# Reordering the borders of block two: squares, sums and sigmoids ahead of splits, another free bank, low parts by halves of features

## The reference

```python
for i in range(2):
    g = norm_gains[i]
    f = swiglu(rmsnorm(h, g[0]), ffn_gate[i,0], ffn_up[i,0], ffn_down[i,0])   # 1024 -> 2816 -> 1024
    h = h + 0.5 * rmsnorm(f, g[1])
    mix = hybrid_mixer(rmsnorm(h, g[2]), ...)      # latent attention (8 heads) and dilated attention (8 heads), w_in, w_out
    h = h + rmsnorm(mix, g[3])
    f = swiglu(rmsnorm(h, g[4]), ffn_gate[i,1], ffn_up[i,1], ffn_down[i,1])
    h = h + 0.5 * rmsnorm(f, g[5])
    gate = sigmoid(rmsnorm(h, g[6]) @ w_ple_gate[i])
    h = h + rmsnorm((p[i] @ w_ple[i]) * gate, g[7])
```

## Time and profile before

| | us |
|---|---|
| median of 3 runs | 2384.09 (2383.19 to 2384.39) |
| the profiled execution's own time | 2383.87 |
| its span, first to last instruction | 2382.6 |
| TensorE busy | 2034.6 (85%) |
| VectorE busy | 959.8 (40%) |
| ScalarE busy | 649.8 (27%) |
| POOL busy | 63.6 (3%) |
| DMA, mean over the span | 272 GB/s |

### The profile page before, as it was taken

One profiled execution on the slowest core, in us unless ns is written; L12 is line 12 of the kernel. 1 busy time (PEld: TensorE's weight loads), 2 busy tenths in 40 slices (PEclk: granted clock), 3 DMA queues, 4 the chain that ended last, 5 costly groups with the idle time before them and its releaser, 6 DMA issues.

```text
span 2382.6 us, 29091 instructions
## 1 busy us (share of the span) xinstructions
PE 2034.6 (85%) x12318; PEld 1354.3 (57%) x12318; DVE 959.8 (40%) x1181; ACT 649.8 (27%) x779; POOL 63.6 (3%) x144
## 2 busy tenths in 40 slices
PE   7999999676666666766688999989999999999998
PEld 4767862111111111111147998769998999778997
DVE  3735431000000000000005656865657666865656
ACT  3423210000000000000004444444444444454434
POOL 0000000000000000000001001000001000000000
PEclk8999999777777777677799999999999999999999
DMA  7345789999999999999995564235554555315552
GB/s 297 119 183 206 280 362 421 420 421 420 420 421 420 420 421 420 421 420 420 421 420 227 191 213 139 107 117 178 200 177 153 192 189 185 128 63 177 201 182 95
DMA packets 91361, 647.46 MB, mean 272 GB/s; under 512 B 10144, under 2 KB 10656, under 8 KB 14304
## 3 DMA queue, kind: packets, MB, share of 16 engines
q1 hardware_dynamic: 91232, 645.61, 69.3%
HBM read 644.52 MB, written 1.05 MB: 271 GB/s over the span
## 4 chain that ended last, share of the span: by engine, by line
PE 53%; DMA 34%; DVE 8%; SPq 2%; ACT 2%; issue 1%; POOL 1%; DVEq 0%; ACTq 0%; POOLq 0%
PE PS L429 13%; PE PS L431 13%; PE PS L430 13%; DMA ring<-in_md 6%; DMA ring<-in_mu 6%; SPq L2704 2%; DMA XT<-in_mu 2%; DMA ahead<-in_mu 2%; PE PS L913 2%; DVE low L1790 2%; PE PS L818 1%; PE PS L784 1%; DMA HRI<-in_md 1%; DMA QT<-in_md 1%; DMA mix<-in_md 1%; DMA XT<-in_md 1%
## 5 line engine op out<-in xcount | busy, mean ns | idle before, releaser
L1790 DVE TENSOR_TENSOR low<-ring,WH 128x2048 fp32r<-128x2048 f32 (+1 forms) x164 | 374.3, 2283 | 189.2 <-ACT WH L2142 186.2
L429 PE MATMUL PS<-XH,WH 128*128 128x256 f32 x1408 | 398.8, 283 | 6.2 <-DVE XL L1808 6.0
L430 PE MATMUL PS<-XL,WH 128*128 128x256 f32 x1408 | 396.9, 282 | 0.0
L431 PE MATMUL PS<-XH,low 128*128 128x256 f32 x1408 | 394.9, 280 | 0.0
L2142 ACT ACTIVATE WH<-ring 128x2048 fp32r<-128x2048 f32 (+1 forms) x164 | 313.1, 1909 | 24.8 <-DMA ring<-in_fg 19.6
L429 PEld LDWEIGHTS PS<-XH,WH 128*128 128x128 f32 x1408 | 266.6, 189 | 10.3 <-issue 8.5
L431 PEld LDWEIGHTS PS<-XH,low 128*128 128x128 f32 x1408 | 269.3, 191 | 0.0
L430 PEld LDWEIGHTS PS<-XL,WH 128*128 128x128 f32 x1408 | 266.5, 189 | 1.4
L1772 DVE TENSOR_TENSOR T1S<-T1S,PS 128x512 f32<-128x512 f32 x16 | 11.0, 688 | 535.9 <-PE PS L878 535.9
L2392 ACT ACTIVATE T1S<-PS 128x512 f32<-128x512 f32 x16 | 9.6, 598 | 546.7 <-PE PS L878 546.6
L878 PE MATMUL PS<-ring,big 128*32 128x512 f32 x616 | 99.7, 748 | 47.1 <-DMA ring<-in_mu 26.9
(11 more groups left out here) (434 smaller groups left out, 3019.9 us busy)
## 6 DMA issues: line engine op xcount, KB each, us to landing
ring<-in_fg SPq DMA_DIRECT2D x44, 1024.0 KB, 4.9
ring<-in_fu SPq DMA_DIRECT2D x44, 1024.0 KB, 4.9
ring<-in_fd SPq DMA_DIRECT2D x44, 1024.0 KB, 4.8
ring<-in_md SPq DMA_DIRECT2D x43, 1024.0 KB, 27.1
ring<-in_mu SPq DMA_DIRECT2D x39, 1024.0 KB, 27.1
ring<-in_mg SPq DMA_DIRECT2D x38, 1024.0 KB, 27.5
ring<-in_wmod SPq DMA_DIRECT2D x24, 1024.0 KB, 6.2
ahead<-in_mg SPq DMA_DIRECT2D x14, 1024.0 KB, 27.4
```

Source lines behind the costliest of these rows:

```text
L429: t.matmul(o, l[0], r[0], start=start, stop=False, skip_group_check=True)
L430: t.matmul(o, l[0], r[1], start=False, stop=False, skip_group_check=True)
L431: return t.matmul(o, l[1], r[0], start=False, stop=stop, skip_group_check=True)
L1790: own(v.tensor_tensor(low[:, w.slot.index, 0:size], w.flat, WH[:, w.slot.index, 0:size].bitcast(f32), ALU.subtract).then_inc(*c.wl.up()), ...
```

## The change

Nothing is computed otherwise; instructions change places in the lists of four engines, with the counts that they wait for.

- Entry, first ffn: ScalarE splits the third tile between its pairs of squares, VectorE right after the products with ROW, the fourth after the factors. TensorE does the product with DG after the second fg tile (first ffn only). The normalised residual is written in step 2 of the ffn. The split of the first fd tile by VectorE goes behind the hidden tile's low part.
- Ffn to mixer: the residual's add comes before the next split and this before the rows on VectorE; ScalarE squares acc(1) before the second split and XR after it. The first dilated product uses bank 0 in place of 6, dilated keys bank 6 in place of 0, kv_up banks 0 and 1 in place of 6 and 7. VectorE does latent(1) before the first rope and the eviction for KT before the second.
- Mixer to ffn: ScalarE squares XR and acc(1) before the second split, the EM copies are spread between, the last behind the high rows; VectorE makes the add of m = 1 before the factor of m = 0 and the second split.
- Gate to the third ffn (l = 0): gains, high rows and sigmoids alternate, the low rows are taken in the order (m, half) (0,0), (1,0), (0,1), (1,1), the first of them between the product and the Newton step of the add; both factors come last; 6 fillings in place of 8.

The diff, cut to its core:

```diff
@@ tensor_program, ffn
-                        if n == 0:
-                            b = (2 * (1 + p) + 1) % 4
+                            if (n, j) == ((0, 1) if f else (1, 0)):
+                                b = (2 * (1 + p) + 1) % 4
...
@@ mixer
-                    x = part(6, 512, 0, j, "wid", 6 * l + j)
+                    x = part(0, 512, 0, j, "wid", 6 * l + j)
...
-                held[6], held[7] = [(c.ds, 4 * l + 1)], [(c.ds, 4 * l + 2)]
+                held[0], held[7] = [(c.ds, 4 * l + 1)], [(c.ds, 4 * l + 2)]
...
-                dilated(1, 0, 0)
+                dilated(1, 0, 6)
+                held[6] = [(c.ds, 4 * l + 3)]
...
-                kv_up(0, 6)
+                kv_up(0, 0)
...
@@ gate
-                    turn_over(4, 8)
+
+                    turned[0, 1], turned[1, 0] = turned[1, 0], turned[0, 1]
+                    held[1], held[2] = held[2], held[1]
+                    turn_over(4, 6)
@@ vector_program: newton, low_rows and factor take ahead=1 for nth(count, ahead); add also meanwhile
-                newton(m)
+                if meanwhile is not None:
+                    meanwhile()
+                newton(m, ahead=ahead)
...
-            for m in range(2):
-                V.wait_ge(c.rw, 2 * m + 2)
...
+            split_to(4)
+
+            def normed_residual():
...
@@ ffn
-                        split_to(tile("fu", 11 * f + n) + 4)
+                        if f or n:
+                            split_to(tile("fu", 11 * f + n) + 4)
...
+                        split_to(tile("fu", 11 * f + n) + 4)
+                        if f == 0 and n == 2:
+                            normed_residual()
@@ mixer
                 add(0, acc(0), 0.5, 4 * l + 1, 22 * l + 9)
+                split_to(tile("wid", 6 * l) + 1)
                 rows(0, 0, gT[:, g0 + 8:g0 + 16])
+                add(1, acc(1), 0.5, 4 * l + 1, 22 * l + 10)
+                split_to(tile("wid", 6 * l) + 2)
                 rows_factor(0)
-                split_to(tile("wid", 6 * l) + 1)
-                add(1, acc(1), 0.5, 4 * l + 1, 22 * l + 11)
-                split_to(tile("wid", 6 * l) + 2)
                 rows(1, 2, gT[:, g0 + 8:g0 + 16])
...
                 rows_factor(1)
-                dilated(0, 0, 6)
                 split_to(tile("wid", 6 * l) + 3)
                 latent(1)
+                dilated(0, 0, 0)
                 split_to(tile("wid", 6 * l) + 4)
-                dilated(0, 1, 7)
...
-                dilated(1, 0, 0)
+                dilated(0, 1, 7)
+                dilated(1, 0, 6)
@@ mixer to ffn
-                for m in range(2):
-                    add(m, acc(m), 1.0, 4 * l + 2, 22 * l + 19 + 2 * m)
-                    if m == 0:
-                        split_to(tile("fg", 22 * l + 11) + 1)
-                    rows(m, 0, gT[:, g0 + 16:g0 + 24])
-                    w, s = factor(2 + m)
-                    spread(m, w, s)
-                    split_to(tile("fg", 22 * l + 11) + 2 + m)
+                add(0, acc(0), 1.0, 4 * l + 2, 22 * l + 19)
+                split_to(tile("fg", 22 * l + 11) + 1)
+                rows(0, 0, gT[:, g0 + 16:g0 + 24])
+                add(1, acc(1), 1.0, 4 * l + 2, 22 * l + 21, 2)
+                w, s = factor(2, 0)
+                spread(0, w, s)
+                rows(1, 0, gT[:, g0 + 16:g0 + 24])
+                split_to(tile("fg", 22 * l + 11) + 2)
+                w, s = factor(3)
+                spread(1, w, s)
+                split_to(tile("fg", 22 * l + 11) + 3)
@@ gate
+                    for j in range(2):
+                        gains(0, j, j, gT[:, 40:48])
+                gated(1, 1)
                 if l == 0:
-                    rows(0, 0, gT[:, 40:48])
-                    w, s = factor(2)
-                    spread(0, w, s)
-                gated(1, 1)
-                add(1, XN[:, 1, :], 1.0, 4 * l + 4)
-                if l == 0:
-                    rows(1, 2, gT[:, 40:48])
-                    w, s = factor(3)
-                    spread(1, w, s)
+                    add(1, XN[:, 1, :], 1.0, 4 * l + 4, meanwhile=lambda: low_rows(0, 0, 0))
+                    for j in range(2):
+                        gains(1, j, 2 + j, gT[:, 40:48])
+                    low_rows(1, 0, 2, 2)
+                    low_rows(0, 1, 1, 0)
+                    low_rows(1, 1, 3)
+                    for m in range(2):
+                        w, s = factor(2 + m)
+                        spread(m, w, s)
+                else:
+                    add(1, XN[:, 1, :], 1.0, 4 * l + 4)
@@ scalar_program: entry, mixer, mixer to ffn
+            split_to(3)
             for m in range(2):
                 sum_square(XN[:, m, :], 2 + m, c.xg, m + 1)
-            split_to(3)
+            split_to(4)
...
-                sum_square(XR[:, 0, :], 2, c.xs, 4 * event + 2)
                 sum_square(acc(1), 1, c.wu, tile("fd", 22 * l + 10) + 1)
                 split_to(tile("wid", 6 * l) + 2)
+                sum_square(XR[:, 0, :], 2, c.xs, 4 * event + 2)
                 latent(0)
...
+                sum_square(acc(0), 0, *pj(l, 6))
+                split_to(tile("fg", 22 * l + 11) + 1)
+                for j in range(2):
+                    rows(0, j, j)
+                sum_square(XR[:, 0, :], 2, c.xs, 4 * event + 2)
+                sum_square(acc(1), 1, c.wu, tile("wo2", 4 * l + 3) + 1)
+                ple_rows(0)
+                split_to(tile("fg", 22 * l + 11) + 2)
+                ple_rows(1)
+                ple_rows(2)
+                for j in range(2):
+                    rows(1, j, j)
+                ple_rows(3)
+                sum_square(XR[:, 1, :], 3, c.xs, 4 * event + 4)
+                split_to(tile("fg", 22 * l + 11) + 3)
...
                 gate(1, 0)
                 if l == 0:
-                    for j in range(2):
-                        rows(0, j, j)
-                    sum_square(XR[:, 0, :], 2, c.xs, 4 * event + 2)
+                    rows(0, 0, 0)
                 gate(1, 1)
+                if l == 0:
+                    rows(0, 1, 1)
                 sum_square(XN[:, 1, :], 1, c.gm, 4 * l + 4)
                 if l == 0:
+                    sum_square(XR[:, 0, :], 2, c.xs, 4 * event + 2)
```

More of the change, by code:

```diff
@@ L1815, in rows, with factor @@
                     low_rows(m, j, b + j)
-            def factor(col):
+            def factor(col, ahead=1):
                 s, u, w = (stat[:, col + 32 * i:col + 32 * i + 1] for i in range(3))
-                V.wait_ge(c.powr, V.nth(c.powr))
+                V.wait_ge(c.powr, V.nth(c.powr, ahead))
                 own(v.scalar_tensor_tensor(w, s, u, s, ALU.mult, ALU.mult))
@@ L1823, in factor, with add @@
                 return w, s
-            def add(m, src, scale, name, squared=None):
+            def add(m, src, scale, name, squared=None, ahead=1, meanwhile=None):
                 V.wait_ge(*W["rows", name].landed)
@@ L1866, in vector_program @@
                 spread(m, w, rr[:, m, 3:4])
-            for m in range(2):
-                V.wait_ge(c.rw, 2 * m + 2)
[L1869 to L1873, removed]
+            split_to(4)
+            def normed_residual():
+                for m in range(2):
+                    V.wait_ge(c.rw, 2 * m + 2)
+                    i = v.tensor_scalar(XR[:, m, :], XN[:, m, :], rr[:, m, 3:4], None, ALU.mult)
+                    if m:
+                        own(i.then_inc(*c.row.up()), c.row)
+                    else:
+                        own(i)
             def ffn(f, p):
@@ L2567, in scalar_program, with ple_rows @@
                 event = 4 * l + 1
[L2568 to L2579 removed]
+                def ple_rows(i):
+                    A.wait_ge(c.ple, 4 * l + i + 1)
+                    own(copy(EM[:, i // 2, (i % 2) * 512:(i % 2) * 512 + 512], PS[:, 2 + i, :]).then_inc(*c.em.up()), c.em)
+                sum_square(acc(0), 0, *pj(l, 6))
[13 more added lines that the diff above has]
+                split_to(tile("fg", 22 * l + 11) + 3)
                 ffn(2 * l + 1, g0 + 16)
@@ L2675, in gpsimd_program @@
             for l in range(2):
-                rsqrt(0, 1, 1024, c.sq)
-                rsqrt(2, 1, 1024, c.sq)
-                rsqrt(1, 1, 1024, c.sq)
+                for col in range(3):
+                    rsqrt(col, 1, 1024, c.sq)
                 rsqrt(4, 2, 128, c.sq)
@@ L2685, in gpsimd_program @@
                 add_normed()
-                if l == 0:
-                    add_normed()
-                else:
-                    for m in range(2):
-                        rsqrt(m, 1, 1024, c.sq)
+                for col in range(4 if l == 0 else 2):
+                    rsqrt(col, 1, 1024, c.sq)
         def sync_program():
```

40 lines of the change are left out of this document (15 added, 25 removed).

## The result

The changed kernel takes 2352.1 us, the median of four runs (2350.99 to 2353.4), against 2384.24 for the kernel before (four runs: the three of the table above and one of 2390.07). The ratio is 0.986, with a 95% interval of 0.9843 to 0.9878. The forecast was 2354.0 us. The profiled execution took 2353.4 us.

What follows compares the result with a forecast made beforehand. Bound: TensorE's waits for VectorE at borders between stages, plus low clock after them. Terms 6.5 + 5.2 + 5.9 + 4.1 + 3.5 + 6.0 = 31.2, less 1.2: 30 off 2383.87, so 2354 us; range 2349 to 2363.

Steps and rivals of the forecast that it cites:

- taken off: Block two: 1.2 us off the gain, for low stretches falling elsewhere in the mixers (1.5 either way) and small unseen waits.
- (a): Ffn to mixer: gains and low rows, now behind low(wid0), come 0.2 to 0.3 us after TensorE wants them.
- (b): Ffn to mixer: low(wid1), factors, latent squares and second-half rows reach TensorE 0.1 to 0.4 us late.
- (c): Ffn to mixer: POOL's pair is held until low(wid2) ends; TensorE waits 0.7 us for the latent instead of 2.2.
- (d): Ffn to mixer: VectorE does a rope before low(wid3), a new TensorE wait of 1.75 us.
- Rival 1: VectorE's splits block POOL's pairs once more in each of six borders: 9 to 14 us back, 2363 to 2368; chance 0.12.
- Rival 2: New waits of 0.6 to 1.75 us at the borders still bring low clock: 9 us back, 2362; chance 0.10.
- Rivals 3 and 4: Borders: waits only change names, 2380 to 2388 us; POOL lockouts at full price, 10 to 20 us slower; 0.03 each.

Runs made afterwards that it cites:

- the filled wait: The kernel before, with 18 filling transposes between the entry's second product and the product with DG: 2384.77 us, ratio 0.9997.

## Why the prediction was right

Terms forecast and what the sections show:

| border | forecast | measured |
|---|---|---|
| entry | 6.5 | 6.48 |
| ffn to mixer, l = 0 | 5.2 | 5.44 |
| mixer to ffn, l = 0 | 5.9 | 5.90 |
| gate to third ffn | 4.1 | 4.03 |
| ffn to mixer, l = 1 | 3.5 | 4.12 |
| mixer to ffn, l = 1, with what lies behind | 6.0 | 7.00 (5.48 and 1.52) |
| taken off | -1.2 | none |
| sum | 30.0 | 32.97 |

*Entry.* With block two 2.47 later, the chain came as worked out: low(fu1) on VectorE at 1286.37 (2.47 after the 1283.9 at which DG was to be ready), the product after RB at 1290.25 with 0.68 (0.6 said), the down product at 1297.34 (1294.85 + 2.47 = 1297.32), its wait 1.20 (1.4 said). What I had wrong here is the price of the low clock. I counted about 2.3 us for it; TensorE's busy time in the section did fall by 2.98, but the filled wait shows that taking away the clock alone is worth 0.3 to 1.0. It was no term of the sum, since I built the forward chain from VectorE's side, and so it did no harm. That 6.48 meets 6.5 to the hundredth is partly luck: with the entry undone in the changed kernel the same distance is 5.79, by where the low stretch fell.

*Ffn to mixer.* At l = 0 the forecast was right by two errors that cancel. New waits at l = 0 came to 2.05 rather than 3.0: of (a) and (b) there is nothing above 0.1, (c) is 0.47 for 0.7, (d) 1.54 for 1.75. Against that the two low stretches cost 2.58 together (208.90 - 206.32), not 3.3, and the old waits were 4.91. 4.91 - 2.05 + 2.58 = 5.44. At l = 1 the same waits, and one stretch of 1.26: 4.12 where 3.5 was said.

*Mixer to ffn and gate.* Waits of 0.28 and 0.28 stand where 0.4 was said; at the gate 0.72 stands where 0.75 was, and 0.34 before the first product, which the prediction didn't name. Idle time fell by 4.13 at l = 0 and the clock gave 1.77. At l = 1 idle time fell by 3.84, not 4.5, and the clock behind the border gave 1.50. The other 1.64 of the 7.00 is the attention's low stretch, 6.8 us before and 3.4 after; it doesn't belong to the border, and without it the section would lie below the forecast.

*The 1.2 taken off* for stretches that might fall worse was the one term without a row behind it, and it had the wrong sign: 1.2 of the 3.0 us between the forecast's sum and the sections. The medians of the runs show 32.1 gained, which is 1.9 us beyond the forecast; where the sections and the medians differ, block one's length is in the medians too.

*Rival 1, POOL locked out.* It happened more often than I had granted and cost little. POOL took 2.60 beside the split at 1279.55 and 2.52 beside that at 1466.17, as well as 1.04 for a 0.19 at (c). TensorE waited for neither of the first two: VectorE itself was in the split that held POOL, and behind the second it stood another 0.50 us for POOL, which TensorE's work covered. Only at (c) can the wait of 0.47 at the latent be put down to it, since that is gone with the split away. The Trainium skill, SBUF — State Buffer, section "SBUF: two separate sides", has the loser of the shared port pair blocked for the whole instruction, and the trace agrees: 0.19 with the split away, 1.04 beside it. *Rival 2, the clock stays low*, had its conditions and didn't come (its 9 us on 2353.9 make 2363, not 2362): neither the changed kernel's new waits of up to 1.54 us nor those of up to 1.61 in the experiments on the order in its mixers brought a low stretch. *Rivals 3 and 4* fell with the sections: idle time went down by 19.9, it didn't change names.

## What to carry to other kernels

Read a border as one forward chain on the engine that TensorE waits for, and order each engine's list by when its result is wanted; a large piece of work that is wanted late (here a 2.29 us split wanted 18 us later) must not stand ahead of small evictions. When a wait goes, work out from the same chain what is late next, since that, not the wait's length, is the gain: 1.53 removed gave 0.6 until the piece behind it moved too. Measure such edits between fixed points of the trace: an unchanged first part that scatters by several microseconds hides effects of 1 to 3 us in the total. Even such a section repeats only to some 0.7 us where a low-clock stretch lies in it.

## What was not expected of the hardware

Ahead of the last microseconds, the low stretches in block two were 3.4, 6.8, 10.2 or 13.7 us long in these profiles. In the attention, where TensorE does small products with gaps of 0.2 to 1.4 us and the code is the same in all kernels, a layer's section was seen with no such stretch, with one of 3.4 (about 1.6 us longer), one of 6.8, and one of 13.7 (another 3.6); five of the experiments on the changed kernel have none at l = 0, where it has one itself. What decides it within these products stays open. And a wait of 2.2 us at the latent brought a low stretch in both layers of the kernel before, but in the version with the mixer undone only at l = 1, so a wait's length alone doesn't tell.
